# Banded attention values on quarters of the array, reordered start and seams, in a two-layer decoder trunk

## What is computed

```python
def trunk(x, ...):
    for l in range(DEPTH):                       # 2 layers
        proj = rmsnorm(x, norm_g[l]) @ w_in[l]
        u, g_main, q_mem, g_mem = split(proj)    # 1024, 1024, 512, 512
        if l < N_A:                              # layer 0: conv4 + real-gated linear recurrence
            y = rglru(causal_conv(u, ...), ...)
        else:                                    # layer 1: banded attention, 16 heads of 64, 2 K/V heads
            kv = rmsnorm(x, kv_norm_g) @ w_kv    # window of 128 keys, with a sink per head
            y = sink_attend(rope(u), k, v, band_mask, sinks)
        om = mem_attend(q_mem, mem_k[l], mem_v[l])   # 4 heads of 128, 256 memory entries
        z = concat([y * silu(g_main), om * silu(g_mem)])
        x = x + z @ w_out[l]
    return rmsnorm(x, final_g), ...
```

## Time and profile before

| | |
|---|---|
| median of three runs | 2077.67 us (2077.16 to 2079.51) |
| the profiled execution | 2079.21 us |
| its span, first to last instruction | 2077.4 us |
| TensorE busy | 2061.9 us, 99% of the span |
| VectorE busy | 1151.5 us, 55% |
| ScalarE busy | 924.0 us, 44% |
| mean granted clock of TensorE | 0.999 of full speed |

### The profile page before, as it was taken

How to read it: one execution, slowest core, us unless ns; L and a number is a source line. 1 busy time by engine, 2 the same in 40 slices (tenths; PEclk the granted TensorE clock), 3 DMA queues, 4 the chain that set the end, 5 groups by cost and what they waited for, 6 DMA issues and landing times.

```text
span 2077.4 us, 32513 instructions
## 1 busy us (share of the span) xinstructions
PE 2061.9 (99%) x13473; PEld 1636.4 (79%) x13473; DVE 1151.5 (55%) x2021; ACT 924.0 (44%) x2015; POOL 15.7 (1%) x26
## 2 busy tenths in 40 slices
PE   9999999999999999999999999999999999999998
PEld 7788887777777777777888888777778778777886
DVE  4845436777767842222634444677778777743232
ACT  5733335777777833222533333344443444422111
POOL 0000000000000000000200000000000000000000
PEclk9999999999999999999999999999999999999999
DMA  9311111111110565344211111222222214475352
GB/s 385 139 64 41 64 39 51 47 61 47 45 51 24 187 216 188 127 155 147 92 44 36 44 39 46 62 75 70 84 70 74 72 56 138 137 261 183 110 187 95
DMA packets 118675, 210.52 MB, mean 101 GB/s; under 512 B 12580, under 2 KB 67908, under 8 KB 113912
## 3 DMA queue, kind: packets, MB, share of 16 engines
q1 hardware_dynamic: 118528, 208.45, 29.9%
HBM read 160.00 MB, written 48.48 MB: 100 GB/s over the span
## 4 chain that ended last, share of the span: by engine, by line
PE 93%; DVE 4%; ACT 1%; DMA 1%; issue 0%; SPq 0%; DVEq 0%
PE bank L597 51%; PE bank L2059 24%; PE bank L1157 3%; PE bank L153 2%; PE bank L701 2%; PE bank L439 2%; PE bank L1146 2%; PE bank L688 2%; PE bank L895 1%; PE bank L617 1%; DMA mk_w<-in_w_mem_kv 1%; DVE wo_lo L1751 1%; PE bank L691 1%; DVE in_x L348 0%; PE bank L1510 0%
## 5 line engine op out<-in xcount | busy, mean ns | idle before, releaser
L597 PE MATMUL bank<-x_hi,w_hi 128*128 128x512 f32 x1600 | 636.2, 398 | 0.0
L597 PE MATMUL bank<-x_hi,w_lo 128*128 128x512 f32 x1600 | 623.6, 390 | 0.0
L597 PE MATMUL bank<-x_lo,w_hi 128*128 128x512 f32 x1600 | 623.3, 390 | 0.0
L597 PEld LDWEIGHTS bank<-x_hi,w_hi 128*128 128x128 f32 x1600 | 300.1, 188 | 98.5 <-issue 38.5
L597 PEld LDWEIGHTS bank<-x_hi,w_lo 128*128 128x128 f32 x1600 | 300.3, 188 | 64.5
L597 PEld LDWEIGHTS bank<-x_lo,w_hi 128*128 128x128 f32 x1600 | 300.5, 188 | 60.4 <-issue 0.7
L2059 PE MATMUL bank<-wo_hi,z_hi 128*128 128x512 f32 x768 | 303.8, 396 | 3.2 <-DVE z_lo L1780 3.2
L2059 PE MATMUL bank<-wo_lo,z_hi 128*128 128x512 f32 x768 | 299.4, 390 | 0.0
L2059 PE MATMUL bank<-wo_hi,z_lo 128*128 128x512 f32 x768 | 299.0, 389 | 0.0
L1193 ACT ACTIVATE it_X<-it_X,stat 128x128 f32<-128x128 f32 x256 | 99.2, 389 | 184.9 <-DVE stat L1262 184.9
L2059 PEld LDWEIGHTS bank<-wo_hi,z_hi 128*128 128x128 f32 x768 | 144.1, 188 | 41.2 <-issue 5.6
(11 more groups left out here) (315 smaller groups left out, 2493.0 us busy)
## 6 DMA issues: line engine op xcount, KB each, us to landing
w_raw<-in_w_items SPq DMA_DIRECT2D x25, 1024.0 KB, 5.1
z_scratch<-it_gz SPq DMA_DIRECT2D x96, 256.0 KB, 2.4
z_raw<-z_scratch SPq DMA_DIRECT2D x32, 768.0 KB, 5.7
it_cs<-in_rope SPq DMA_DIRECT2D x32, 512.0 KB, 4.2
wo_raw<-in_w_out SPq DMA_DIRECT2D x6, 2048.0 KB, 9.5
in_rows<-in_x_prompt SPq DMA_DIRECT2D x4, 2048.0 KB, 28.2
in_x<-in_x_T SPq DMA_DIRECT2D x4, 2048.0 KB, 25.9
z_x<-in_x_prompt SPq DMA_DIRECT2D x16, 512.0 KB, 5.4
```

Source lines behind the costliest of these rows:

```text
L597: last = nc.tensor.matmul(ps, s_, r_, start=(k == 0 and q == 0), stop=(k == KT - 1 and q == 2))
```

## The change

- The values of the banded attention are done on quarters of the array: for each query block and head, the two halves of the 128 keys are matmuls of their own, on 64 rows and 64 columns. The lower key half of the block before is needed only by the first 64 queries, the upper key half of the own block only by the last 64. The key halves are added up in two banks, T0 and T1; `swa_result` adds the two. The samples of this stage move from T1 to S3, with a wait for the maximum of the chunk whose scores are there, and the scores wait for their evacuation.
- On TensorE the scores of chunk q-1 come ahead of the flips of chunk q-2; on VectorE the maximum comes ahead of the rope.
- At the start the third memory item is done in two halves, with the first spread between them; it goes to banks 0 and 1, the fourth item to bank 7. Its weights are loaded in two halves, one ahead of the first columns, one behind. The sample columns have a semaphore of their own. The first activation is a square root instead of a copy.
- In the last memory head of each layer a half of the next item's `weights_low` comes behind the maximum.
- In layer 0's output VectorE splits tile 0 between two pairs of output weights, and flip(0) is done inside the next half.
- In layer 1's output the two weights ahead of step 31's `swa_weights` go to the end of that step, `final_g` is loaded earlier in SP's queue, and a square root stands at the beginning of ScalarE's part.

```diff
...
-    mm_ld0, first_half = sem("mm_ld0"), mk_ld[4]
+    mm_ld0, first_half, xs_ld, third_half = sem("mm_ld0"), mk_ld[4], mk_ld[5], mk_ld[6]
...
-    mk_bank = lambda i: m.bank[(4, 5, 0, 1, 5, 5, 5, 5)[i]]
+    mk_bank = lambda i: m.bank[(4, 5, None, 7, 5, 5, 5, 5)[i]]
...
         s.dma_start(w[0][:, half(1), :], A["w_mem_kv"][0][:, half(1)]).then_inc(mk_ld[0], 16)
-        s.dma_start(mt[:, :, M:NM], A["xs_T"]).then_inc(mm_ld, 16)
+        s.dma_start(mt[:, :, M:NM], A["xs_T"]).then_inc(xs_ld, 16)
         load_w(1)
-        load_x(0)
-        load_w(2)
+        load_rows(0)
+        s.dma_start(w[2][:, half(0), :], A["w_mem_kv"][2][:, half(0)]).then_inc(third_half, 16)
+        load_columns(0)
+        s.dma_start(w[2][:, half(1), :], A["w_mem_kv"][2][:, half(1)]).then_inc(mk_ld[2], 16)
...
         act.wait_ge(ids, 2)
-        nc.scalar.activation(st[:, 63:64], m.eps, ACT.Copy)
+        nc.scalar.activation(st[:, 63:64], m.eps, ACT.Sqrt, bias=m.eps, scale=1.0)
...
         memory_gain(0, range(0, 4))
-        act.wait_ge(mm_ld, 32)
+        act.wait_ge(mm_ld, 16)
         memory_gain(0, range(4, KT))
+        act.wait_ge(xs_ld, 16)
...
         v.wait_ge(mk_done, i + 1)
-        src = mk_bank(i).rearrange("p (t c) -> p t c", t=2)
+        src = m.psum[:, 0:2, 0:256] if i == 2 else mk_bank(i).rearrange("p (t c) -> p t c", t=2)
...
+    def third(pe, part):
+
+        pe.wait_ge((third_half, mk_ld[2])[part], 16)
+        for k in range(4 * part, 4 * part + 4):
+            for h in range(2):
+                last = nc.tensor.matmul(m.bank[h][:, 0:256], mg[0][k][:, 128 * h:128 * h + 128], w[2][:, k, :], start=(k == 0), stop=(k == KT - 1))
+        if part:
+            last.then_inc(mk_done, 1)
...
         if i:
-            pe.wait_ge(mk_ld[i], 32 if i == 4 else 16)
+            pe.wait_ge(mk_ld[i], 32 if i in (4, 5, 6) else 16)
...
         memory_sums()
+        third(pe, 0)
         spread(pe, 0)
-        memory(pe, 2)
+        third(pe, 1)
...
         X, PTs = buf("X", [128, 8, W], 39936), buf("PTs", [128, 2, 2, CH], 31744)
+        ysum = buf("ysum", [128, CH], 52224)
...
     sample_bank = lambda kind, w: S2 if kind == "kv" and w == 1 else row_bank[kind]
-    row_bank = {"kv": S3, "mem": S3, "main": S3 if l == 0 else T1}
+    row_bank = {"kv": S3, "mem": S3, "main": S3}
...
         mem_max(v, chn, *MEM[q])
+        if q == G - 1:
+            weights_low(v, item("mem", *MEM[q][:2]) + 1, halves[1])
...
                 behind(v, chn, q)
-            if c in (2, 3):
+            if c in (2, 3) and q < G - 1:
...
             pe.wait_ge(S["z_ready"], B["z_ready"] + G + q)
-        if q == 0 or (q % 4 == 3 and q < NQ - 8):
-            pe.wait_ge(S["n_free"], B["n_free"] + NMH + (q + 1) // 4 + 4)
...
             pe.wait_ge(S["z_ready"], B["z_ready"] + G)
-            pe.wait_ge(S["n_free"], B["n_free"] + NMH + 3)
...
+        if q % 4 == 0 and q < NQ - 4:
+            pe.wait_ge(S["n_free"], B["n_free"] + NMH + q // 4 + 4)
...
         for t in range(4):
-            for kt in range(2):
-                for h in range(2):
-                    last = nc.tensor.matmul(T0[64 * h:64 * h + 64, t * 128:(t + 1) * 128], kV[:, 4 * c + t + kt, 64 * h:64 * h + 64],
-                                            PTs[:, h, kt, t * 128:(t + 1) * 128], start=(kt == 0), stop=(kt == 1))
+            for part in range(2):
+                for r in range(2):
+                    kt, n = 1 - (part ^ r), (128, 64)[part]
+                    o = t * 128 + (64 if part and r else 0)
+                    for h in range(2):
+                        last = nc.tensor.matmul((T0, T1)[r][64 * h:64 * h + 64, o:o + n], kV[64 * r:64 * r + 64, 4 * c + t + kt, 64 * h:64 * h + 64],
+                                                PTs[64 * r:64 * r + 64, h, kt, o:o + n], start=(part == 0), stop=(part == 1))
...
                 mem_flip(pe, *MEM[-1])
+            if 1 <= q <= NQ:
+                swa_scores(pe, q - 1)
...
                 swa_flip(pe, q - 2)
-            if 1 <= q <= NQ:
-                swa_scores(pe, q - 1)
...
                 swa_values(pe, q - 2)
-            if q < NQ and q % 4 == 0:
+            if q < NQ - 4 and q % 4 == 0:
+                if q:
+                    pe.wait_ge(S["m_ready"], B["m_ready"] + G + q)
...
-    def swa_result(v, q):
+    def swa_result(v, chn, q):
         v.wait_ge(S["o_done"], B["o_done"] + G + q + 1)
-        gate_result(v, "main", *ipc(q), T0)
+        g = chunk("main", *ipc(q))
+        v.wait_ge(S["gz_free"], B["gz_free"] + g + 2)
+        z = gz[g % NG][:, :]
+        nc.vector.tensor_tensor(ysum[:, :], z, T1, ALU.mult)
+        chn.link(nc.vector.tensor_tensor(z, z, T0, ALU.mult))
+        nc.vector.tensor_tensor(z, z, ysum[:, :], ALU.add).then_inc(S["z_ready"], 1)
...
                 mem_head(v, chn, G - 1)
-            ahead["ahead_of_dve"](v, q)
...
                 swa_weights(v, q - 2)
+            if 1 <= q <= NQ:
+                swa_max(v, chn, q - 1)
...
                 swa_rope(v, chn, q)
-            if 1 <= q <= NQ:
-                swa_max(v, chn, q - 1)
...
             if q >= 2:
-                swa_result(v, q - 2)
+                swa_result(v, chn, q - 2)
...
         if q == 31:
-            weights_low(v, 1)
+            weights_low(v, 1, range(0, 2))
             split_dve(v, 0)
+            weights_low(v, 1, range(2, 4))
...
                 load_x(s, t)
+            s.dma_start(fg[:, :], A["final_g"].unsqueeze(0).broadcast_to([128, D])).then_inc(fgl, 16)
...
-
-    def ahead_of_dve(v, q):
-        if q == 31:
-            weights_low(v, 1, range(0, 2))
...
         if q == 31:
-            weights_low(v, 1, range(2, 4))
+            weights_low(v, 1)
...
-    ahead = dict(early_sp=early_sp, late_sp=late_sp, ahead_of_dve=ahead_of_dve, within_act=within_act, behind_act=behind_act, within_dve=within_dve, behind_dve=behind_dve, weights_sp=ahead_weights_sp, tiles_sp=ahead_tiles_sp, rows_sp=ahead_rows_sp, weights_act=ahead_weights_act,
+    ahead = dict(early_sp=early_sp, late_sp=late_sp, within_act=within_act, behind_act=behind_act, within_dve=within_dve, behind_dve=behind_dve, weights_sp=ahead_weights_sp, tiles_sp=ahead_tiles_sp, rows_sp=ahead_rows_sp, weights_act=ahead_weights_act,
...
     def sync(s, finish):
-        if l == 1:
-            s.dma_start(fg[:, :], A["final_g"].unsqueeze(0).broadcast_to([128, D])).then_inc(fgl, 16)
...
     def scalar(act, last):
+        if l == 1:
+            nc.scalar.activation(st[:, 63:64], m.eps, ACT.Sqrt, bias=m.eps, scale=1.0)
...
                 last.then_inc(mmd, 1)
+            if l == 0 and (t, h, k) == (1, 1, 1):
+                flip(pe, 0)
...
                     half(pe, t, h)
-                if l == 0 and h == 0 and t >= 1:
+                if l == 0 and h == 0 and t >= 2:
```

## The result

| | before | after | ratio, 95% interval |
|---|---|---|---|
| median | 2077.53 us (4 runs, 2077.16 to 2079.51) | 2067.27 us (4 runs, 2066.90 to 2067.98) | 0.9949 [0.9932, 0.9966] |
| profiled execution, its span | 2079.21, 2077.4 | 2066.90, 2065.1 | |

The time lies inside the predicted range of 2058 to 2070 us, 4.0 us above the predicted 2063.3 and just outside the forecast's own range (to 2066.5). The sum had promised 14.4 us from profile to profile; the spans differ by 12.3.

What follows compares the result with a forecast made beforehand. TensorE was taken as the bound, busy 2061.9 of 2077.4 us. Terms 12.5 + 3.6 + 0.65 + 0.1 + 0.9 + 1.3 - 4.6 = 14.4 us gave a median of 2063.3; own range 2060 to 2066.5, wider range 2058 to 2070.

Steps and rivals of the forecast that it cites:

- Values on quarters: Banded stage on TensorE: values run falls from 1.90 to about 1.52 us, 0.39 saved a chunk, 12.5 us over 32 chunks.
- Scores ahead of flips at nothing: Banded stage on TensorE: the same tile-shape changes in another order cost nothing, with 0.05 us a chunk kept to both sides.
- Steady state has no new stall: Banded stage: moved waits for samples and VectorE's result longer by 1.34 us a chunk stay hidden, at no cost.
- The margin of 0.9 us: VectorE per banded chunk: at most 13.8 us of work with a weight split against a cycle of 14.7.
- The 2 us that the prediction counted: Banded stage: the maximum that the samples' products need is done 2 us before TensorE asks.
- The start: Kernel start: split third item and reordered loads let the first projection begin at 39.8 instead of 43.4, 3.6 us saved.
- The 1.7 us for the granted clock: Start: without idle gaps the half-clock stretch from 27.1 to 30.4 goes, returning 1.7 us on TensorE.
- The last three steps: End of layer 1's banded stage: VectorE's longer result is not hidden, 5.8 us new idle minus 1.2, so 4.6 lost.
- The predicted 1.6 for a weight: Step 31: output weights are no longer two ahead, so TensorE's second part, needing one per 0.68 us, loses 1.6 us.
- Seams: Between stages: 0.65 and 0.1 from weight splits, 0.2 and 0.7 in layer 0's output, 1.3 in layer 1's.
- 1.3 us of the final gain: Layer 1's output: final_g and the square root's table are in early, so z_lo(2) is no longer late, 1.3 us saved.
- Profile and median: Whole kernel: 14.4 us off the profiled 2079.2 gives 2064.8; taken as 1.5 above the median, this gives 2063.3.

Runs made afterwards that it cites:

- quarters alone: Kernel before plus only the values on quarters, the result in three operations and the samples' other bank, with all orders and the start as before; 2073.08 us, ratio 0.9979.
- old start: Changed kernel with the whole start of the kernel before: third memory item in one piece, old load order, table load at 22.8 us; 2069.12 us, ratio 0.9957.
- z load early: Changed kernel with the fourth tile's z load in the second layer's output put ahead of the sample rows' 13 loads on SP's queue; 2067.10 us, ratio 0.9948.
- rope first: Changed kernel with the rotation of the queries ahead of the maximum again on VectorE in the banded stage; 2074.01 us, ratio 0.9983.

## Why the prediction was right, and where its sum was off

**Values on quarters** (12.5 us for 32 chunks at 0.39): right. The run fell by 0.40, the second part's width alone makes the difference, and quarters do run four at a time. The Trainium skill's page "TensorE: Matmul & The Clock Gate", section "Wait — 56ns, not 53.3ns?", states a floor of about 25 ns between starts. In this run four starts lie within 20 ns, so here that floor does not hold between passes in different quarters of the array; nothing in this kernel tells whether it holds within one.

**Scores ahead of flips at nothing** (0.05 to both sides): no cost was put into the sum, and it has one. In the steady part it is 0.03 to 0.04 us a chunk, 0.9 to 1.0 us in all, within the 0.05 kept to both sides. In the last steps the order delays VectorE's start by 1.25 us, which the dates of the prediction contain but which was never priced against the old order. Undone, it gives 2.0 to 2.3 us.

**Steady state has no new stall**: right, but by the maximum's new place, to which the prediction gave no part, so this is luck: with the rotation in front the kernel is at 2074 us, outside the range. The margin of 0.9 us left out that VectorE waits for ScalarE's sums within a step (1.30 us with quarters alone). With the maximum in front the rotation fills that wait. The 2 us that the prediction counted between the maximum and the samples' products were right: with the rotation in front the maximum comes 2.7 us later, and TensorE waits 0.81 for it in each of six chunks.

**The start** (3.6): the two first profiles show 3.65, but over all profiles it is about 2.4, and the run with the old start puts 1.9 to 2.2 on it. The 1.7 us for the granted clock was real in the earlier trace rows: all three profiles with the old start have a stretch at 0.50 there (in one of them at 12 us), and none of the nine with the new one has.

**The last three steps** (4.6 lost): right in size. The lead fell by 3.9 between the values of chunk 29 and 31, against 4.6 less 0.8 for two runs on quarters. The waits for z_lo(0) and z_lo(1) are 1.82 and 1.77, predicted 1.9 each. The predicted 1.6 for a weight was there too, in two shapes. In the changed kernel the granted clock is half behind the first wait (stretches of the changed kernel; the clock is the value behind POOL's "(x0)"):

```profile
1763.00:1766.50 3.50, 1.68 (x22) 1.30 (x15) 3.40 (x8) 3.25 (x18) 0.00 (x0) 0.99 1.03 374
1766.50:1769.90 3.40, 3.40 (x10) 2.64 (x9) 3.29 (x7) 3.40 (x6) 0.00 (x0) 0.50 1.15 352
1769.90:1773.30 3.40, 3.40 (x63) 2.68 (x68) 3.37 (x5) 2.77 (x3) 0.00 (x0) 1.00 0.82 325
```

With the z load early and with the old start the same wait of 1.8 us was followed by the full clock, and four waits for weights came that the changed kernel does not have. Timeline of TensorE, z load early:

```profile
1774.89 0.50 PE L2084 MATMUL bank<-wo_hi,z_hi 128*128 128x512 f32 x1 [0.28 <-DVE wo_lo L1776]
1776.03 0.50 PE L2084 MATMUL bank<-wo_hi,z_hi 128*128 128x512 f32 x1 [0.17 <-DVE wo_lo L1776]
1777.16 0.50 PE L2084 MATMUL bank<-wo_hi,z_hi 128*128 128x512 f32 x1 [0.16 <-DVE wo_lo L1776]
1778.30 0.50 PE L2084 MATMUL bank<-wo_hi,z_hi 128*128 128x512 f32 x1 [0.17 <-DVE wo_lo L1776]
```

These starts are 1.14 us apart, VectorE's time for a weight, where TensorE needs 0.68. From the end of the first z_lo wait to the first matmul behind these four weights, TensorE takes 12.13 us in the changed kernel (1765.15 to 1777.28), 12.15 with the z load early (1766.95 to 1779.10) and 10.45 before (1780.24 to 1790.69). So 1.7 us are lost either way, and the slower clock took nothing on top: without it TensorE would have waited for VectorE.

**Seams**: the weight split behind layer 0's last memory head gave 0.63 (0.65 predicted; the lead goes from 3.87 to 4.50 there, 0.2 of it having come since the first projection). Layer 0's output gave 0.31 instead of 0.9 (4.50 to 4.81): the flip gave 0.47 (predicted 0.7), and at the low half at 724, which VectorE bounds as predicted, the lead fell by 0.16 (4.50 to 4.34) where 0.2 more were to stay. The wait of 1.1 there is VectorE's date, which TensorE now reaches sooner. In layer 1's output the 1.3 us of the final gain came, and 0.8 was lost at z_lo(3). Its row on SP's queue, and who waits for it:

```profile
1807.63 5.91 SPq L1444 DMA_DIRECT2D sm_rows<-srow_scratch  x13
...
1814.92 0.43 SPq L1784 DMA_DIRECT2D z_raw<-z_scratch  x1
```

```profile
1822.75 1.49 ACT L1800 ACTIVATE z_hi<-z_raw 128x1536 fp32r<-128x1536 f32 x1 [11.82 <-DMA z_raw<-z_scratch]
```

```profile
1826.09 0.50 PE L2081 MATMUL bank<-wo_hi,z_hi 128*128 128x512 f32 x1 [0.83 <-DVE z_lo L1804]
```

The load was held behind thirteen others by the first tile's result, as before; with the 1.3 us gained ahead of it, TensorE reached it first. The prediction named what a removed stall makes late next in other places, and not in this one.

**Profile and median.** Of the 14.4 us, 12.3 show between the two profiles: about 1.0 was lost to the reordering, 0.8 to z_lo(3), and 0.3 is left for the seams and the start. The medians differ by 10.3. The profiled execution of before lay 1.7 above its median, that of after 0.4 below; the prediction took the first for a constant. About 1.2 of the 2.0 is the start by the averages above. The rest was not traced, for only profiled executions have a trace.

## What to carry to other kernels

- Price a reordering by what it delays on the engine that starts its step with the moved result, at the place where that engine has no slack left, not by the mover's own edges.
- Where one edit lengthens an engine's work and another reorders it, run them apart: here one order paid for the longer result and the other cost 2 us, and the whole change hid both.
- A wait that depends on the first loads varies by 2 us between executions. Take its worth from the medians of a run with that part undone.

## What the hardware showed that was not expected

- While GpSimd works on two inputs in SBUF (2.7 us on average for 128x1024), VectorE's operations with two inputs in SBUF are held until it ends: 0.16 became 2.34 us, 0.69 became 2.47 to 2.88, 1.23 became 3.08. Two that had begun before GpSimd's operation kept their 1.23, and there GpSimd's took 3.37 instead of 2.33 to 2.42. Operations with an input in PSUM or with one input kept their time beside it in the same stretches (0.68 for each of the four products from PSUM, 1.22 for the reduction, 0.20 for the reciprocal). The Trainium skill's page "GPSIMD Engine Reference", section "8. Key points", says that the two share their interfaces and that VectorE's instructions with two SBUF inputs contend; the rows agree, and add that the small operation pays as much as the large.
- After idle waits of 1.8 us at the same place the granted clock fell to 0.5 in both profiles of the changed kernel and in that of rope first, and stayed at 1.0 in those of the z load early and of the old start. The second wait of 1.7 to 1.8 us, some 18 us later, left it at 1.0 in all of them. With quarters alone a wait of 2.9 us (to 1771.09) left it at 1.0, and one of 2.0 (to 1814.38) was followed by 0.5. So the length of a wait alone does not tell whether it is paid for twice.
